# Reordering around turned rows, a gate slab's low part and the last early block in a two-block transformer kernel

## The reference, cut to what matters

```
def first_block(x, c, ...):                     # 2 layers
    for l in range(2):
        shift1, scale1, gate1, shift2, scale2, gate2 = split(silu(c) @ w_ada[l] + b_ada[l])
        h = rms_norm(x, norm1_g[l]) * (1 + scale1) + shift1
        q, k, v, conv..., pool_x = split(h @ w_in[l])
        mix = concat(windowed_gqa(q, k, v), short_conv(...), multiscale_pool(...)) @ w_out[l]
        x = x + gate1 * mix
        h2 = rms_norm(x, norm2_g[l]) * (1 + scale2) + shift2
        x = x + gate2 * peer_ffn(h2)            # 8 heads, product keys
    return x

def peer_ffn(h):                                # for each token and head
    s1, s2 = scores against 128 keys each;  v1, i1 = top_k(s1, 16);  v2, i2 = top_k(s2, 16)
    top = 16 best of v1 + v2;  expert = i1 * 128 + i2;  gate = softmax(top)
    y = sum over chosen experts of gate * gelu(h . u[expert]) * v[expert]

def second_block(x, ...):                       # 2 layers
    for l in range(2):
        h = rms_norm(x)
        dq, dk, dv, mq, mk, mv, c_q, c_kv, k_pe, g = split(h @ w_in[l])
        oa = differential attention(dq, dk, dv);  ob = block attention(mq, mk, mv)
        q = rms_norm(c_q) @ w_uq;  kv = rms_norm(c_kv) @ w_ukv;  oc = latent attention(q, kv, k_pe)
        mixed = sum over the 3 branches of sigmoid(g) * (branch @ w_branch)
        x = x + rms_norm(mixed @ w_out[l])
        u = relu(rms_norm(x) @ w_up[l]) ** 2
        x = x + rms_norm(u @ w_down[l])
```

## Time and profile before

| | |
|---|---|
| median of 3 runs | 3178.02 us |
| lowest and highest | 3173.62, 3184.35 us |
| the profiled execution's own time | 3177.01 us |
| its span, first to last instruction | 3175.2 us |
| mean granted TensorE clock | 0.96 of full speed |
| instructions | 48,964 |
| read from HBM, written | 519.44 MB, 3.16 MB (165 GB/s over the span) |

### The profile page before, as it was taken

One profiled execution on the slowest core, in us unless ns is written; L12 is line 12 of the kernel. 1 busy time (PEld: TensorE's weight loads), 2 busy tenths in 40 slices (PEclk: granted clock), 3 DMA queues, 4 the chain that ended last, 5 costly groups with the idle time before them and its releaser, 6 DMA issues.

```text
span 3175.2 us, 48964 instructions
## 1 busy us (share of the span) xinstructions
PE 2966.4 (93%) x17330; PEld 2580.8 (81%) x17330; DVE 1990.0 (63%) x3635; ACT 1314.1 (41%) x2096; POOL 271.3 (9%) x387
## 2 busy tenths in 40 slices
PE   8997899999999988978999999998998998999898
PEld 4674798999999865877999999997876887977797
DVE  4669866777777633887666666665546654646564
ACT  1235843444444412565444444444333433433332
POOL 0026600000000000563000000000000000000000
PEclk9898999999999997999999999998999898999899
DMA  7532156666666631303555566554324454324354
GB/s 304 208 113 80 41 185 207 230 231 228 225 230 230 209 148 53 140 8 117 188 185 185 195 192 195 192 183 157 128 107 165 154 186 154 128 112 163 121 182 146
DMA packets 130791, 524.30 MB, mean 165 GB/s; under 512 B 17965, under 2 KB 28077, under 8 KB 108009
## 3 DMA queue, kind: packets, MB, share of 16 engines
q1 hardware_dynamic: 120632, 508.13, 46.6%
q10 hardware_dynamic: 10034, 14.52, 1.4%
HBM read 519.44 MB, written 3.16 MB: 165 GB/s over the span
## 4 chain that ended last, share of the span: by engine, by line
PE 44%; issue 7%; ACT 3%; DVE 2%; DMA 1%; ACTq 0%; DVEq 0%; PEld 0%; POOL 0%; PEldq 0%; POOLq 0%; SPq 0%
PE prob_ps L1239 10%; PE acc L1251 10%; PE acc L924 7%; PE acc L909 3%; PE acc L1452 3%; PE acc L1467 3%; PE acc L1408 2%; PE acc L1433 1%; PE turn_ps L1017 1%; ACT arena L1778 1%; PE acc L991 1%; ACT arena L1768 1%; PE prob_ps L1002 0%; ACT slab L1770 0%; PE turn_ps L937 0%
## 5 line engine op out<-in xcount | busy, mean ns | idle before, releaser
L1239 PEld LDWEIGHTS prob_ps<-hTr,utr 128*128 128x128 f32 x5856 | 737.4, 192 | 32.7 <-issue 14.9
L1239 PE MATMUL prob_ps<-hTr,utr 128*128 128x256 f32 x5856 | 748.5, 284 | 8.2 <-DVE arena L2542 3.5
L1251 PE MATMUL acc<-vr,wtr 128*128 128x512 f32 x2964 | 718.8, 391 | 1.3 <-DVE vr L2519 1.3
L1251 PEld LDWEIGHTS acc<-vr,wtr 128*128 128x128 f32 x2964 | 541.0, 188 | 104.1 <-issue 1.9
L2519 DVE TENSOR_TENSOR vr<-slab,vr 128x1024 fp32r<-128x1024 f32 x246 | 301.4, 1225 | 405.9 <-ACT vr L1812 405.6
L1812 ACT CAST vr<-slab 128x1024 fp32r<-128x1024 f32 x246 | 258.2, 1050 | 576.0 <-PE acc L1251 568.2
L2494 DVE TENSOR_TENSOR utr<-slab,utr 128x1024 fp32r<-128x1024 f32 x244 | 297.2, 1218 | 14.4 <-ACT utr L1795 14.4
L1795 ACT CAST utr<-slab 128x1024 fp32r<-128x1024 f32 x244 | 255.4, 1047 | 9.0 <-issue 4.8
L2071 POOL TENSOR_TENSOR small<-small 128x2 f32<-128x2 f32 (+3 forms) x18 | 20.8, 1155 | 2744.3 <-DVE small L2143 1466.2
L2766 DVE TENSOR_TENSOR slab_lo<-slab,w_hi 128x2048 fp32r<-128x2048 f32 x64 | 143.8, 2288 | 127.7 <-ACT w_hi L2043 127.7
L2043 ACT CAST w_hi<-slab 128x2048 fp32r<-128x2048 f32 x64 | 119.2, 1907 | 163.2 <-DMA slab<-in_pack_b 152.8
(11 more groups left out here) (292 smaller groups left out, 4182.5 us busy)
## 6 DMA issues: line engine op xcount, KB each, us to landing
slab<-in_pack_b SPq DMA_DIRECT2D x132, 1024.0 KB, 4.9
slab<-in_peer_v SPq DMA_DIRECT2D x255, 512.0 KB, 3.4
slab<-in_peer_u SPq DMA_DIRECT2D x244, 512.0 KB, 4.7
arena<-in_pack_a SPq DMA_DIRECT2D x84, 512.0 KB, 4.9
slab<-in_pack_a SPq DMA_DIRECT2D x40, 1024.0 KB, 7.0
arena<-in_peer_u SPq DMA_DIRECT2D x6, 1024.0 KB, 14.3
slab<-in_pack_b SPq DMA_DIRECT2D x4, 832.0 KB, 6.0
arena<-in_pack_a SPq DMA_DIRECT2D x2, 1024.0 KB, 18.6
```

The costliest lines, as they stand in the source:

```text
L1239: ins = pe.matmul(prob_ps[:, m % 2, 0:S], utr[:, m % 2, uh, k * P:k * P + P], hTr[:, hh, k, :], start=(k == 0 and n == 0), stop=(k == KD - ...
L1251: ins = pe.matmul(y_ps[:, t, n, :], wtr[:, m % 2, wh, t * P:t * P + P], v[:, vh, n * 512:n * 512 + 512], start=first and k == 0, stop=last ...
```

## The change

It moves steps in the engines' orders and adds none that computes anything new. In the second block: the wait for the low part of the last turned normed rows stands before the second set of eight products of `dq` and of `up0`, not before the first (`proj_T`'s argument `low`); the low part of `g2` is made ahead of the waits for the banks of `ukv0` and `ukv1`; and the mixed rows are turned in two halves, `mx_0` and `mx_1` inside the last accumulator of the branches, `mx_2` and `mx_3` inside the first of `w_out`, with a signal of `mix_ready` for each half and VectorE's low parts of rows and slabs put in that order. In the first block: in the second layer the pairs are turned ahead of the last early block, the exponential runs ahead of the gelu of block 8, and the gelu of the last block behind the one-hot rows of turn 1; in the first layer the waits for the last gates stand behind the first two `activations`, `u_high(0)` ahead of the last copy of gates and `u_low(0)` ahead of the wait; in the second layer TensorE's wait for them stands before `combine(0)` as before. The tile is cleared four experts earlier (five turns of the loop, then the memset, then four experts written out), and the load of the bias row is issued inside SyncE's loop over the plain experts.

```diff
-        mix_ready = Signal(sem("mix_ready"), a=1, b=4)
+        mix_ready = Signal(sem("mix_ready"), a=1, b=5)
...
                         sp.wait_ge(*wt_ready.at("a", l, PLAIN - 2))
                         sp.sem_inc(passed["sp"], 1)
+                        sp.wait_ge(tiles_clear, 2)
+                        sp.dma_start(next_row[0:1], io["b_ada"][l + 1:l + 2, 0:512]).then_inc(bias_row_in, 16)
...
-                sp.wait_ge(tiles_clear, 2)
-                sp.dma_start(next_row[0:1], io["b_ada"][l + 1:l + 2, 0:512]).then_inc(bias_row_in, 16)
...
                         for n, (wp, hp) in enumerate(HALVES):
+                            if h == 0 and j == 0 and n == 1:
+                                wait_turned("b", l, *low)
...
+                def turn_pairs():
+                    pe.wait_ge(*pairs_ready.at("a", l, 1))
+                    pe.wait_ge(*picked.at("a", l, POOLC))
+                    turn("a", l, "pairs0", [pairs[:, i, t, :] for i in range(2) for t in range(T)])
+                    pe.wait_ge(*pairs_ready.at("a", l, 2))
+                    turn("a", l, "pairs1", [pairs[:, 2, t, :] for t in range(T)])
+                if not EARLY[l]:
+                    turn_pairs()
                 for i in range(EARLY[l]):
+                    if i == EARLY[l] - 1:
+                        turn_pairs()
...
-                pe.wait_ge(*gates_kept.at("a", l, S // TOKG))
-                pe.wait_ge(*accs.emptied_at("a", l, "s3"))
                 wait_turned("a", l, "pairs0", "pairs1")
...
                 if EARLY[l]:
+                    pe.wait_ge(*gates_kept.at("a", l, S // TOKG))
...
                     activations(0, 0)
                     activations(1, 1)
+                    pe.wait_ge(*gates_kept.at("a", l, S // TOKG))
                     combine(0, 0, first=True)
...
-                wait_turned("b", l, "h_2", "h_3")
-                proj_T(l, "dq")
+                pe.wait_ge(*h_hi.at("b", l, 4))
+                proj_T(l, "dq", low=("h_2", "h_3"))
...
+                def mixed_turned(first):
+                    pe.wait_ge(*mix_ready.at("b", l, 4 + first // 2))
+                    for g in (first, first + 1):
+                        turn("b", l, f"mx_{g}", [bn[:, t, (2 * g + c) * P:(2 * g + c + 1) * P] for c in range(2) for t in range(T)])
...
+                            if c == NB - 1 and n == 1 and t == 0:
+                                mixed_turned(0)
                         ins.then_inc(accs.full_sem("b", use), 1)
...
-                pe.wait_ge(*mix_ready.at("b", l, 4))
-                turn_rows("b", l, "mx_", bn)
-                wait_turned("b", l, "mx_2", "mx_3")
+                wait_turned("b", l, "mx_0", "mx_1")
...
+                            if n == 0 and h == 0 and t == 0:
+                                mixed_turned(2)
+                        if n == 0 and h == 0:
+                            wait_turned("b", l, "mx_2", "mx_3")
...
-                wait_turned("b", l, "hm_2", "hm_3")
+                pe.wait_ge(*hm_hi.at("b", l, 4))
...
+                                if u == 0 and j == 0 and n == 1:
+                                    wait_turned("b", l, "hm_2", "hm_3")
...
+                for i in range(EARLY[l] - 1):
+                    if i == 4:
+                        candidates(PH - 1)
+                    if i == 8:
+                        gates_exp()
+                    early_gelu(i)
+                if not EARLY[l]:
+                    gates_exp()
...
                 one_hot(0)
                 for n in range(S // TOKG):
                     if n + 1 < S // TOKG:
                         one_hot(n + 1)
+                    if n == 0 and EARLY[l]:
+                        early_gelu(EARLY[l] - 1)
+                    if n + 1 == S // TOKG and not EARLY[l]:
+                        u_high(0, 0, 0)
                     gates_out(n)
...
-                dve.wait_ge(*gates_kept.at("a", l, S // TOKG))
...
                 if not EARLY[l]:
                     u_low(0, 0)
+                dve.wait_ge(*gates_kept.at("a", l, S // TOKG))
...
-                    with dve.Fori(0, PLAIN // 4) as it:
+                    with dve.Fori(0, PLAIN // 4 - 1) as it:
                         four(it * 4 + 3)
                     dve.drain()
                     dve.memset(next_row, 0.0).then_inc(tiles_clear, 1)
+                    four(PLAIN - 1)
...
+                proj_rest(18, 19)
                 dve.wait_ge(*accs.emptied_at("b", l, "ukv0"))
                 dve.wait_ge(*accs.emptied_at("b", l, "ukv1"))
                 dve.sem_inc(passed["dve"], 1)
-                proj_rest(18, 19)
...
                 mixed(2, 0)
                 late_low(6)
+                mixed_low(0, 1)
                 mixed(2, 1)
+                late_low(7)
+                mixed_low(2, 3)
+                late_low(8, 9)
```

More of the change, by code:

```diff
@@ L896, in _, with proj_T @@
             hT_r = (hT_hi, hT_lo)
-            def proj_T(l, name):
+            def proj_T(l, name, low=()):
                 u0 = 2 * PROJ.index(name)
@@ L1206, in _ @@
                     ins.then_inc(early_full, 1)
-                pe.wait_ge(*pairs_ready.at("a", l, 1))
-                pe.wait_ge(*picked.at("a", l, POOLC))
-                turn("a", l, "pairs0", [pairs[:, i, t, :] for i in range(2) for t in range(T)])
-                pe.wait_ge(*pairs_ready.at("a", l, 2))
-                turn("a", l, "pairs1", [pairs[:, 2, t, :] for t in range(T)])
                 pe.wait_ge(*accs.emptied_at("a", l, "s2"))
@@ L1780, in _ @@
                 act.wait_ge(*turns.emptied_at("a", l, "pairs0"))
-                one_hot(0)
-                for n in range(S // TOKG):
-                    if n + 1 < S // TOKG:
-                        one_hot(n + 1)
-                    gates_out(n)
                 def u_high(i, m, place):
@@ L1795, in u_high @@
                     act.copy(utr[:, m % 2, 0], expert_u[:, m % 2]).then_inc(ut_act.sem, 1)
+                one_hot(0)
+                for n in range(S // TOKG):
+                    if n + 1 < S // TOKG:
+                        one_hot(n + 1)
+                    if n == 0 and EARLY[l]:
+                        early_gelu(EARLY[l] - 1)
+                    if n + 1 == S // TOKG and not EARLY[l]:
+                        u_high(0, 0, 0)
+                    gates_out(n)
                 def gelu(i, m):
@@ L1812, in v_high @@
                     act.copy(v_place(l, i)[:, 0], v_raw(l, i, m)).then_inc(v_hi.sem, 1)
-                if not EARLY[l]:
-                    u_high(0, 0, 0)
                 act.wait_ge(*htr_lo.at("a", l, 1))
```

30 lines of the change are left out of this document (14 added, 16 removed).

## The result

The changed kernel took 3126.75 us (median of 4 runs, 3124.66 to 3129.32), the kernel before 3179.06 in the same comparison (3173.62 to 3184.35). The ratio is 0.9836, with a 95% interval of 0.9817 to 0.9855: 52 us less, between 46 and 58. Forecast were 3135 us, a range of 3124 to 3150, and a sum of 43.0 us. Both the time and the sign are as forecast; the gain is 9 us larger than the sum.

The account below looks back on a forecast made before the run. TensorE, busy 93% of the span, was taken as the bound, losing time to holes and slow matmuls behind them. Terms 10.8 + 13.4 + 2.8 + 3.8 + 5.0 + 7.2 = 43.0 us gave 3135 us against the median, range 3124 to 3150.

Parts of the forecast that it names:

- g2: Third gate slab, second block: earlier low part closes a 3.5 us hole and returns 1.87 us of clock; 10.8 us in all.
- Mixed rows: Second block, branches to w_out: turning in two halves takes 24.3 us instead of 30.3; 6.0 and 7.4 us, together 13.4.
- Normed rows: Second block, first product of normed rows, four times: each start moves up by 0.7 us; 2.8 us in all.
- End of the gates: First block, first layer: hole before the activations shrinks from 3.47 to 1.3 us, then full speed; 3.8 us.
- Bias row cleared earlier: End of the plain experts' loop: the memset wait of 3.54 us goes and 1.5 us of clock returns; 5.0 us.
- Pairs: First block, second layer: earlier turning, hidden exponential and last early block's cover bring gates forward; 7.2 us, 5.4 at low clock.
- clock not given back: Rival: the clock's share behind closed holes is not regained, or falls elsewhere; 10 us lost, 3145 us; chance 0.14.
- half hidden: Rival, mixed rows: ScalarE's copy stands behind a late slab's cast, each layer losing 3 us; 3141 us; chance 0.08.
- slab loads: Rival, second block: TensorE moves up against the loads and half the 27 us gain is given back; 3148 us; chance 0.07.
- table loads: Rival, second-layer gates: three ScalarE table loads for Relu and Square under gelu's table, 3.8 us; 3139 us; chance 0.03.
- the load for each one-hot: Rival, second-layer gates: each Relu and Square needs another table, 64 loads, 82 us slower; 3217 us; chance 0.02.
- no effect: Rival, whole kernel: other engines end together at the holes and new equal waits appear; 3178 us; chance 0.02.

Follow-up runs that it names:

- e7: Kernel before, with 24 unread products filling each of three TensorE holes (before g2 in both layers, before the cleared-tile wait): 3174.07 us, ratio 0.9986.
- e8: Changed kernel, but the second half of the mixed rows is turned ahead of w_out's first product: 3140.89 us, ratio 0.9884 against the kernel before.
- e4: The kernel before once more, unchanged, for a second trace: 3179.17 us in a single run.
- e6: Kernel before, with only the wait for the last turned normed rows' low part moved behind the first eight products, four times: 3179.51 us, ratio 0.9996.
- e1: Kernel before plus only the earlier pair turning, earlier exponential and late gelu in the first block's second layer: 3169.13 us, ratio 0.9974.
- e9: Kernel before plus 9 unread products ahead of the last expert of the first block's first layer: 3171.58 us, ratio 0.9980.
- e10: Changed kernel plus 19 unread products ahead of the last expert of the first block's first layer: 3139.26 us, ratio 0.9879 against the kernel before.
- e12: Changed kernel plus unread identity products in the four holes before the second block's normed rows, 20 in the first, 34 in the others: 3114.87 us, ratio 0.9795.
- e11: Changed kernel plus 56 unread identity products in each of the four holes before the second block's normed rows: 3137.69 us, ratio 0.9874.

## Why the prediction was right, and where its size was off

- *g2*: foreseen 5.4 us a layer, measured 5.5 and 5.4. Right, hole and clock; e7 shows the clock's share by itself. In one point the prediction read its rows too strongly: the 24 products in 4.45 us were not all at 1.2 GHz, since the granted clock over them was 0.62 (the row beside e7), so about a quarter of the time was at the full clock. The price was taken from the rows and is not touched by it.
- *Mixed rows*: foreseen 6.0 and 7.4, measured 6.2 and 7.7 from the end of the branches to the end of w_out, 24.1 us in both layers for the 24.3 foreseen. Right step by step. e8 shows that both halves are needed. That the layers differ was a draw of the clock: e4 has the slow w_out in the first layer as well. All six traces with this edit as it stands have 24.1 us in both layers, while the seven with the old order have 30.3 to 32.4. So the edit is worth 6.2 to 8.4 us a layer, 7.5 in the mean of these fourteen layers, and 13.9 us was a low draw of the kernel before.
- *Normed rows*: foreseen 4 x 0.7 = 2.8, measured 1.3 in e6. This is the term whose step failed: "each start moves up by 0.7 us" held, and the end did not follow, since these products run at the low clock until a rise that does not come earlier. The sum took the full clock for them without looking at the rows behind. In the traces of the changed kernel the first three places gave 0.1 to 0.5 us each, as in e6, but the last gave 2.8 us in both, since there the clock rose sooner, so that these traces have 3.8 and 3.3 us in all. That the term then looks large enough is luck and not its step.
- *End of the gates*: foreseen 3.8, measured 3.8, with the full clock behind a hole that was cut to 1.2 us.
- *Bias row cleared earlier*: foreseen 5.0, measured 5.3, and no expert of the four was late.
- *Pairs*: foreseen 7.2, measured 8.1 at the first copy of gates and 7.6 in e1; the hidden exponential, the cover by the last early block and the absence of table loads all as told. The 0.9 us over come ahead of the gates: the turnings started right behind the eleventh block, and the one-hot rows at 1347.03, which is 1364.7 on the scale of before, where 1365.6 was foreseen. By the rule of the Trainium skill, "ScalarE: Activation LUTs", section "Table sets: the hidden batching unit", that cheap functions such as relu are in every set, no load was due for the Relu under gelu's table; the timeline has none, neither for it nor for the Square.
- *The sum*: the edits' own terms measure 10.9 + 13.9 + 1.3 + 3.8 + 5.3 + 8.1 = 43.3 us, for 43.0. With the mean of the mixed rows (2 x 7.5) they are 44.4. The remaining 9 us of the first trace are the 8.4 us from the last experts to the early blocks, 2.5 more at the normed rows, and smaller ones of both signs elsewhere (1.6 gained in the second block's scores, 2.2 lost in the first experts behind the gates, 1.5 in the branches). The prediction counted the clock only behind the holes that the edits close. It did not count that other stages meet the clock differently, although it named "the clock's slow stretches turn up elsewhere" as a way to be wrong; they turned up to the good side, and that is luck. A fair account, an estimate from these rows, is that about 44 us belong to the mechanisms and the rest to the clock at places that no edit touches, with the 3.5 us by which the medians of before differ between comparisons as its uncertainty.
- *Rivals*: clock not given back is out by e7, half hidden by e8, slab loads by the chain without a hole from the branches to w_out's end, table loads and the load for each one-hot by the timeline, no effect by the result.

What stays open is what decides over the clock in stages with many short waits. The added work in e9 and e10 changed it at many later places, and the time since the start does not settle it. One place and two amounts of added work were tried, one in each kernel. Whether what counts is the shift itself or what TensorE did just before was not separated.

## What to carry to other kernels

Where one engine is busy for nine tenths, list its holes, and price each as the hole plus the matmuls behind it that run at the low clock; but look in the rows whether the clock has risen by then: products that started earlier below the rise gave more than half of it back (e6). Move the producer, not the wait: a low part queued behind a wait it doesn't need, or a turning that needs only half of the sum, cost several us each and nothing to move. And when a kernel has stages with many short waits, a change of 10 us is only known after several traces: here 1.1 us of useless work made one kernel 6 us faster.

## What the runs showed of the hardware that was not expected

- The same 142 products with the same waits took 32.2 to 40.9 us by the granted clock (0.89 to 0.58), and this differed between kernels that are the same up to there (32.2 to 38.2 in five of them). A change upstream that has nothing to do with the stretch brought the shortest times to the kernel before (e7 and e9, 32.5).
- Filling holes with products that nobody reads keeps the clock up and pays if the filling ends in time: 3114.87 us with the filling fitted (e12), 3137.69 with 22 to 36 products more in each hole (e11).
- A 128-column f32 product of the identity took 0.23 us at the full clock (e11), twice a turning of the same size (0.79 us for eight); it is recorded as two matmuls.
